# Local attention of a hybrid layer: the block transposes become products with a diagonal matrix of reciprocal row sums

## What is computed

```
s = jnp.einsum('bnqhgd,bnkhd->bnhgqk', qb, kk) * (D ** -0.5)
s = jnp.where(valid, s, -1e30)
p = jax.nn.softmax(jnp.concatenate([s, sink], axis=-1), axis=-1)[..., :-1]
o = jnp.einsum('bnhgqk,bnkhd->bnqhgd', p, vv)
```

## Time and profile before

| | |
|---|---|
| time, median of 3 runs | 2103.79 us (2102.29 to 2104.71) |
| profiled execution, its own time | 2098.76 us |
| span of the profiled execution | 2096.8 us |
| mean granted TensorE clock | 0.981 |
| PE, DVE, ACT busy | 1991.4, 1089.2, 959.2 us |
| `mix`, first layer | from 189.7 us to about 297 us of the span |
| `mix`, second layer | from 516.6 us to about 620 us of the span |

### The profile page before, as it was taken

How to read it: one execution, slowest core, us unless ns; L and a number is a source line. 1 busy time by engine, 2 the same in 40 slices (tenths; PEclk the granted TensorE clock), 3 DMA queues, 4 the chain that set the end, 5 groups by cost and what they waited for, 6 DMA issues and landing times.

```text
span 2096.8 us, 25344 instructions
## 1 busy us (share of the span) xinstructions
PE 1991.4 (95%) x9889; PEld 1484.4 (71%) x9889; DVE 1089.2 (52%) x2023; ACT 959.2 (46%) x1758; POOL 12.7 (1%) x28
## 2 busy tenths in 40 slices
PE   8999889999889999899999999999999999999997
PEld 4876446677456788566788888777666668888885
DVE  5623864632873422656665543452386575555343
ACT  4734764743674233574433222254587543232223
POOL 1000000000000000000000000000000000000000
PEclk8999999999989999999999999999999999999999
DMA  8431432223202433003233333325400123333331
GB/s 281 124 92 51 161 101 80 61 72 91 81 21 81 144 95 88 16 1 116 70 92 100 92 95 101 107 62 124 146 2 2 51 71 101 92 100 96 96 93 48
DMA packets 301267, 183.13 MB, mean 87 GB/s; under 512 B 17550, under 2 KB 292108, under 8 KB 299948
## 3 DMA queue, kind: packets, MB, share of 16 engines
q1 hardware_dynamic: 295437, 166.05, 27.2%
q10 hardware_dynamic: 4704, 13.31, 1.7%
q0 software_dynamic: 1008, 2.15, 0.3%
HBM read 179.22 MB, written 2.27 MB: 87 GB/s over the span
## 4 chain that ended last, share of the span: by engine, by line
PE 84%; DVE 8%; ACT 5%; issue 1%; DMA 1%; ACTq 0%; DVEq 0%
PE PS L902 22%; PE PS L904 22%; PE PS L903 22%; PE PS L1048 3%; PE PS L1076 2%; PE PS L1061 2%; DVE SE L2152 1%; PE PS L1202 1%; DVE WLO L2078 1%; PE PS L1014 1%; DVE X L2045 1%; PE PS L1120 1%; ACT WHI L1514 1%; PE PS L1225 1%; PE PS L1234 1%
## 5 line engine op out<-in xcount | busy, mean ns | idle before, releaser
L903 PE MATMUL PS<-LO,WHI 128*128 128x512 f32 x1690 | 659.7, 390 | 0.0
L902 PE MATMUL PS<-HI,WHI 128*128 128x512 f32 x1578 | 626.3, 397 | 24.9 <-DVE LO L2051 10.2
L904 PE MATMUL PS<-HI,WLO 128*128 128x512 f32 x1578 | 616.0, 390 | 0.0
L2078 DVE TENSOR_TENSOR WLO<-RING,WHI 128x1024 fp32r<-128x1024 f32 (+3 forms) x271 | 314.5, 1161 | 528.8 <-ACT WHI L1514 527.8
L1514 ACT ACTIVATE WHI<-RING 128x1024 fp32r<-128x1024 f32 (+3 forms) x271 | 272.7, 1007 | 468.2 <-PE PS L904 446.1
L902 PEld LDWEIGHTS PS<-HI,WHI 128*128 128x128 f32 x1578 | 297.2, 188 | 108.3 <-issue 26.8
L903 PEld LDWEIGHTS PS<-LO,WHI 128*128 128x128 f32 x1690 | 318.5, 188 | 65.0 <-issue 1.7
L904 PEld LDWEIGHTS PS<-HI,WLO 128*128 128x128 f32 x1578 | 297.1, 188 | 62.7
L902 PE MATMUL PS<-HIDDEN,WHI 128*128 128x512 f32 x352 | 137.1, 389 | 0.6 <-PE PS L904 0.6
L903 PE MATMUL PS<-HIDDEN,WHI 128*128 128x512 f32 x352 | 137.0, 389 | 0.0
L904 PE MATMUL PS<-HIDDEN,WLO 128*128 128x512 f32 x352 | 136.9, 389 | 0.0
(11 more groups left out here) (341 smaller groups left out, 2325.2 us busy)
## 6 DMA issues: line engine op xcount, KB each, us to landing
RING<-in_ffn_w_up SPq DMA_DIRECT2D x88, 512.0 KB, 3.7
RING<-in_w_in SPq DMA_DIRECT2D x48, 512.0 KB, 3.8
RING<-in_w_mod SPq DMA_DIRECT2D x32, 512.0 KB, 4.3
RING<-in_ffn_w_down SPq DMA_DIRECT2D x32, 512.0 KB, 4.0
RING<-in_ev_w_in SPq DMA_DIRECT2D x30, 512.0 KB, 3.8
RING<-in_w_out SPq DMA_DIRECT2D x16, 512.0 KB, 4.5
RING<-in_od_w_in SPq DMA_DIRECT2D x15, 512.0 KB, 3.8
RING<-in_ffn_w_down SPq DMA_DIRECT2D x16, 384.0 KB, 3.4
```

The costliest lines, as they stand in the source:

```text
L902: mm(bank, WHI[i2][:, i, :], hi, start=(k == 0), stop=False)
L903: mm(bank, WHI[i2][:, i, :], lo, start=False, stop=False)
L904: return mm(bank, WLO[i2][:, i, :], hi, start=False, stop=last)
L2078: tt(WLO[i2][:, 0:nk, :], raw, WHI[i2][:, 0:nk, :], ALU.subtract).then_inc(me.signals(w_split), 1)
```

## The change

The transpose of a block of exponentials E by the identity becomes a product of the same block with diag(1 / row sum), so the result is transposed and normalised at once. The diagonal matrices of a pair (two of 128x128) are written by one DVE instruction behind the reciprocals, into a part of the buffer S that was unused in this stage (`DIAG`). The two `normalise` instructions of a pair go from ACT. PE's `turn` waits for the DVE instruction, and no longer for ACT.

```diff
+        DIAG = S.rearrange("p a t -> p (a t)")[:, 1544:2312].rearrange("p (r a q) -> p r a q", r=3, a=2)
...
                 def turn(i):
                     nb = todo[i]["n"] // B
-                    pe.wait_ge(swa_probs, 2 * (n0 + i + 1))
+                    pe.wait_ge(swa_probs, n0 + i + 1)
...
-                            ins = nc.tensor.transpose(PS[:, 4, (a * nb + c) * B:(a * nb + c + 1) * B],
-                                                      pair_e(i % 3, a, 2 * B)[:, c * B:c * B + B], IDN)
+                            ins = mm(PS[:, 4, (a * nb + c) * B:(a * nb + c + 1) * B],
+                                     pair_e(i % 3, a, 2 * B)[:, c * B:c * B + B], DIAG[:, i % 3, a, :], start=True, stop=True)
...
-                def normalise(i):
-                    n, r = todo[i]["n"], i % 3
-                    act.wait_ge(swa_recip, n0 + i + 1)
-                    for a in range(2):
-                        e = pair_e(r, a, n)
-                        fn(e, e, ACT.Copy, scale=RDEN[:, 2 * r + a:2 * r + a + 1]).then_inc(me.signals(swa_probs), 1)
                 for i in range(MIX_SLOTS):
-                    if 0 <= i - 1 < len(todo):
-                        normalise(i - 1)
...
                     nc.vector.reciprocal(RDEN[:, 2 * r:2 * r + 2], DEN[:, 2 * r:2 * r + 2]).then_inc(me.signals(swa_recip), 1)
+                    dve.wait_ge(*me.last)
+                    tt(DIAG[:, r], IDN.unsqueeze(1).broadcast_to([P, 2, P]), RDEN[:, 2 * r:2 * r + 2].unsqueeze(2).broadcast_to([P, 2, P]),
+                       ALU.mult).then_inc(swa_probs, 1)
```

## The result

The changed kernel takes 2107.47 us (median of 20 runs), the kernel before on the same chip 2102.04 us (20 runs): ratio 1.0022, 95% interval [1.0012, 1.0032]. It is slower by 4.6 us, with 2.5 to 6.7 us inside the interval. The forecast was 8.2 us: the sign is right, the size too large. The profiled execution took 2102.12 us, 3.4 us more than that of before. Behind the second `mix` the profiled executions differ by up to 6 us with the very same program there (1475 to 1482 us), so the medians, and not two profiles, say what the change costs.

A forecast was written before the change was run, and what follows sets the result against it. No engine is saturated; the chain passing between PE, DVE and ACT bounds the mix stages. Stage delays of 3.4 (or 1.1) + 5.9 give 9.3 (or 7.0), middle 8.2 us; from 2103.79 to 2112.0 us, range 2102 to 2119.

The forecast's parts named there:

- The terms: Per pair with two key blocks: ACT loses 0.79 us, DVE gains 0.47 us, PE gains 0.51 us.
- Step (a): Slots 0 to 4, PE and DVE taking turns: additions lie on the chain, slot 5's retention mask 2.7 us late.
- The walk: Row-by-row following of the delay through both mix stages: 3.4 (or 1.1) us late in the first, 5.9 in the second.
- Step (b): Slots 5 to 10, DVE without gaps: each pair adds 0.47 us, lag growing from 2.7 to 5.7 us.
- Step (c): From slot 11, chain through PE, ACT and DVE: a round costs 0.4 us, ACT's cut being smaller than the additions.
- The tail of the first stage: Slots 15 to 17: PE's last steps 3.4 us late, or 1.1 if L1202's twelve products run at full clock.
- The step that failed: Second stage: three half-clock stretches of 7 or 8 us kept as in before, the walk ending 5.9 us late.
- rival 2: Products and shorter waits for ACT hold PE's clock up: 2102 us, with half of that 2107; chance 0.17.
- Rival 1: Turns were the bound: 18.6 us of waits for normalise vanish, PE adds 14, so 2099.2 us; chance 0.06.
- Rival 3: Longer waits for DVE bring one or two more half-clock stretches, some 3.5 us each: 2115 to 2119 us; chance 0.13.
- Rival 4: PE's additions lie in its idle time, only DVE's lag counts: some 4 us, 2108 us; chance 0.08.

The follow-up runs named there:

- r1: The kernel before, unchanged, profiled a second time: 2103.09 us.
- r3: The kernel before, unchanged, profiled a third time: 2105.94 us.
- r2: The changed kernel, unaltered, profiled a second time: 2112.32 us.
- y2: The changed kernel with four extra products ahead of three scores a stage: 2101.54 us, ratio 0.9985 to before.
- y1: The kernel before with five extra transposes ahead of the turns that waited for ACT: 2098.28 us, ratio 0.9965.
- z2: The changed kernel with ten extra transposes ahead of five scores a stage and five ahead of the last turn: 2103.47 us, ratio 1.0014 to before.
- z1: The kernel before with five extra transposes ahead of eight turns and five scores a stage: 2095.4 us, ratio 0.9974.
- x1: The kernel before with plain products by the identity as turns, ACT still normalising: 2110.28 us, ratio 1.0039.
- s1: z1 with plain products by the identity in place of transposes as turns: 2105.84 us, ratio 1.002 to before.
- x3: The changed kernel with turns as transposes again, diagonals still written, output not normalised: 2105.92 us, ratio 1.0017 to before.
- x2: The kernel before without ACT's two normalise instructions a pair, output not normalised: 2093.45 us, ratio 0.9954.
- x4: The kernel before with three extra products ahead of the turns that waited for ACT: 2099.26 us, ratio 0.9979.
- s3: The changed kernel with the diagonal behind the next pair's scores and five extra transposes ahead of five scores and the last turn: 2095.37 us, ratio 0.9973 to before.
- z3: y4 with seven extra transposes ahead of five scores a stage and five ahead of the last turn: 2097.87 us, ratio 0.998 to before.
- y3: The kernel before with the 32 normalise instructions of a stage on GpSimd instead of ACT: 2124.88 us, ratio 1.0096.
- y4: The changed kernel with the diagonals written by GpSimd instead of DVE: 2098.41 us, ratio 0.9974 to before.

## Why the prediction came out too large

**The terms held.** Products +0.51 us per four blocks: 0.58 became 1.09. The diagonal: 0.46 measured, 0.47 forecast. The Trainium skill's factor of four for the transpose mode ("TensorE: Matmul & The Clock Gate", section "Terms") is not borne out by this trace, which has 1.9.

**Step (a)** said 2.7 us at slot 5; the mask and the reciprocals there came 1.75 us late. The kernel before has its slots 4 and 5 at half clock (first line, 1.7 us lost), the changed one has its stretch only at 225 to 229 us (second line):

```profile
211.00:215.00 4.00, 4.00 (x19) 1.66 (x20) 1.17 (x6) 2.53 (x5) 0.00 (x0) 0.57 0.00 0
```
```profile
225.00:229.00 4.00, 3.98 (x24) 1.96 (x23) 3.93 (x11) 1.05 (x3) 0.00 (x0) 0.57 0.32 126
```

The walk carried before's durations over as if the stretch stayed. r1 has no stretch ahead of slot 5, and shows what the step costs at full clock; here are its first scores and the reciprocals of pair 5:

```profile
186.55 0.49 PE L1120 MATMUL PS<-Z 64*128 64x128 f32 x4 [0.73 <-ACTq L1964]
```
```profile
215.48 0.15 DVE L2223 RECIPROCAL TINY<-TINY 128x2 f32<-128x2 f32 x1
```

That is 28.93 us behind the start of the stage; in both profiles of the changed kernel it is 32.32. So the step costs 3.4 us at full clock, more than the walk said, and the stretch that before had there and the changed kernel didn't gives 1.6 us of it back.

**Step (b)** said 0.47 a pair, and it is: from pair 9 to 10 the lag grows from 3.60 to 4.08 us. One of the five steps, where DVE waited 0.23 us before, added only 0.16. With pair 10's own diagonal the shift at the end of slot 10 is 3.8 + 0.46 = 4.3 us instead of 5.7: 0.95 of the difference is from (a), 0.3 is this slack, which I had counted as none, and 0.2 is a slip in the sum: six pairs at 0.47 on top of 2.7 make 5.5. At full clock the lag would be 3.4 us at pair 5, 2.0 more by pair 10 (27.67 us instead of 25.63 between the two) and 0.46 for its diagonal, 5.9 in all: there the walk comes out right because two errors cancel.

**Step (c)** said that a round costs 0.4 us rather than giving anything back: from pair 11 to pair 14 the shift goes from 2.9 to 3.3 us. DVE's wait for the exponentials shrank from 2.69 to 1.33 us and stayed.

**The tail of the first stage** had two values, 3.4 us, and 1.1 if the twelve products of L1202 came out at full clock. They did (the changed kernel, PE, slot 15):

```profile
277.57 0.66 PE L1142 MATMUL PS<-ET,Z 128*64 128x128 f32 x8 [0.25 <-ACT H L1717]
278.16 2.77 PE L1203 MATMUL PS<-RING,TINY 128*32 128x512 f32 x12
```

and the stage became 0.9 us longer (106.45 to 107.37). Taking the middle of both put 1.2 us into the sum. The other profiles say that even 0.9 is too much for this stage: r1 and r3, with more of it at half clock, have 111.6 and 110.0 us, r2 has 108.3.

**The step that failed** is the one that left the half-clock stretches of before where they were. It shows most plainly in the second stage, where the walk said 5.9 us and assumed that the three stretches of the earlier trace rows stay. The stage became 3.5 us longer (102.46 to 105.94). Counted from the stage's start, the reciprocals are 5.0 us late at pair 5 (3.4 by the step, 1.6 by the changed kernel's own stretch at 542 us), 7.0 at pair 10 and 5.3 at pair 15. The 5.9 of the walk is nearly reached by then. The last turn starts 4.5 us late (611.53 against 604.73, less 2.33), and waits for its diagonal, as forecast:

```profile
611.53 1.16 PE L1130 MATMUL PS<-S,E 128*128 128x128 f32 x8 [1.90 <-DVE S L2218]
```

So the tail gave back 1.8 us between the last reciprocals and the end, where the walk had nothing: it is there that before has its third stretch. Before lost 10.2 us to the clock in this stage (in r1 and r3 12.0 and 10.2), the changed kernel 5.1 (in r2 8.5). The stretch at 603 to 611 us, 3.4 us lost, is in all three profiles of before, and its place runs at full clock in both of the changed kernel, though r2 has a shorter one right behind it.

So it was the forecast and a part of rival 2 together: the walk's cost is there, and a good part of it is paid back by the clock. Single profiles say so three times. With the lost us taken off, the stages of the changed kernel are 206.3 us and those of before 194.6: 11.7 us, an upper figure, since a slow PE costs nothing while it waits for others. With the lighter fillers the same difference is 9.1 us (y2 against y1), and with the clock held equally in both it is 8.5 (z2 against z1). The times agree in direction only: z2 against z1 costs 8.1 us with an uncertainty of 3.4, where without filler the change costs 4.6 with one of 2.1, and the two ranges overlap. Rival 2's own argument, that the changed kernel's longer waits for DVE speak against it, was half right: these waits did bring stretches of their own (542, 576, 593 us), but shorter ones, 4 us where before had 7. I had named the effect, priced it (10 us for the whole) and given it 0.17 instead of working a part of it into the sum.

**Rival 1** (turns were the bound) is refuted by the time, which rose, and by the 16.2 us of waits for scores that came instead. **Rival 3** is not seen in the medians; r2's extra stretch, at 2112.32 us, shows one execution that has it. **Rival 4** came nearest in size (2108) but its mechanism, PE's additions lying in idle time, isn't the cause: x1 and s1 show these additions at 8.2 and 9.7 us.

**What stays open.** How the difference between the parts' sum, 11.8 us, and the 4.6 us of the whole divides between the clock and the products that lie in waits for DVE (4.7 us less wait than in x3) is not settled, as the intervals are 2 to 4 us wide on either side. Nor is it shown why a stretch lasts 4 us in one place and 7 in another.

**What the turns are made of** may matter too. The expectation of x3 named a sign: if products hold the clock up and transposes don't, x3 has more at half clock than the changed kernel. It has, 13.7 us against 6.8 and 10.2, and before, with transposes, loses 13.7 to 22.2. But x1, all of whose turns are products, loses 10.2, as much as x2, all of whose turns are transposes, and products also keep PE busy for 14 us more. The Trainium skill ("TensorE: Matmul & The Clock Gate", section "Part 4: PE-mode transpose") says that for transposes the full clock does not engage; that speaks for rival 2. Against it, five transposes in the waits did as much (y1, 0.9965, 6.8 us lost) as three products (x4, 0.9979, 8.5 us lost). So the filled waits show that PE's standing still is a part of what brings the stretches here; whether turns of products help besides is open, as every run with products in the turns also has longer turns.

## What to carry to other kernels

Work that goes from an idle engine to the chain that two busy engines form costs time there, even if the waits for the idle one head the list: ask of each such wait what stands next behind it. The cure here was the place, not the amount: with the diagonal behind the next pair's scores (0.9989), or on GpSimd, idle in this stage (0.9974), the change no longer costs anything. Against the kernel before with filled waits it gains nothing either: 0.9973 (s3) and 0.998 (z3) stand beside 0.9974 (z1) and 0.9965 (y1). And where the kernel before has stretches at half clock, a walk must be made twice, with them and without, and the forecast be weighed between the two. One profile is too few for that: the first stage of before lost 3.4, 10.2 and 6.8 us in its three.

## What the runs showed of the hardware

- Filler in waits pays though it is pure extra work: 5.2 us of transposes in the second stage and 3.7 in the first gave -7.4 us by the ratio (y1).
- Executions of one program lose different amounts to the clock: 13.7, 22.2 and 17.1 us in the two stages of before, at the same main places in the second stage and at other ones in the first. The whole times, 2098.76, 2103.09 and 2105.94 us, don't follow that order.
- Where the granted clock is the same, executions repeat each other almost exactly: the reciprocals of pair 5 stand 28.93 us behind the start of the stage in three of the six stages of before, and 30.47, 30.55 and 30.57 us in the three that have 1.7 us lost ahead of them.
- On GpSimd a TENSOR_SCALAR of 128x256 float32 with a per-partition factor takes 1710 ns (605 ns for 128x128, y3), more than twice a TENSOR_TENSOR of 128x256 (737 ns, y4), which DVE does in 0.42 us.
